# The last expert pass of a mixture-of-experts step: its gate and up products in two column halves, in two PSUM banks

## What is computed

```
h = silu(einsum('td,edf->tef', xf, w_gate)) * einsum('td,edf->tef', xf, w_up)
h = h * gates[..., None]              # gates: two of 32 experts for each token
y = einsum('tef,efd->td', h, w_down)  # f = 256, d = 1024
yp = rms_norm(yp + y, norm_f)         # and the same for the sample rows
```

## Time and profile before

| | us |
|---|---|
| median of 3 runs (613.83 to 614.82) | 614.73 |
| the profiled execution, its whole time | 613.61 |
| its span in the trace (first to last instruction) | 612.0 |
| TensorE busy in the span | 587.9 |
| last pass, first gate and up product | 577.30 |
| copy of the last pass's output (`yo`) begins | 590.10 |
| last scaling on VectorE begins | 608.05 |

### The profile page before, as it was taken

How to read it: one execution, slowest core, us unless ns; L and a number is a source line. 1 busy time by engine, 2 the same in 40 slices (tenths; PEclk the granted TensorE clock), 3 DMA queues, 4 the chain that set the end, 5 groups by cost and what they waited for, 6 DMA issues and landing times.

```text
span 612.0 us, 9005 instructions
## 1 busy us (share of the span) xinstructions
PE 587.9 (96%) x2880; PEld 350.1 (57%) x2880; DVE 322.5 (53%) x725; ACT 234.5 (38%) x415; POOL 52.6 (9%) x126
## 2 busy tenths in 40 slices
PE   7999999999999999999999989999999998999985
PEld 4876796867777686777656744343333333333331
DVE  4648788867767686767735873531141111121137
ACT  6451417275664737475535340211111211112224
POOL 1200001000000000000000002131112121121100
PEclk9999999999999999999999999999999999999999
DMA  8431308922223133221299989999999999999995
GB/s 315 137 137 71 138 34 323 408 104 69 77 77 103 43 103 109 71 77 69 79 331 391 384 348 322 364 419 419 419 418 421 419 421 419 421 420 417 415 370 222
DMA packets 34412, 157.65 MB, mean 258 GB/s; under 512 B 6480, under 2 KB 6864, under 8 KB 22992
## 3 DMA queue, kind: packets, MB, share of 16 engines
q1 hardware_dynamic: 28768, 146.51, 61.0%
q0 software_dynamic: 5472, 10.63, 4.7%
q10 hardware_dynamic: 144, 0.15, 0.1%
HBM read 151.87 MB, written 14.17 MB: 271 GB/s over the span
## 4 chain that ended last, share of the span: by engine, by line
PE 76%; DMA 10%; DVE 6%; ACT 3%; SPq 2%; issue 2%; DVEq 0%; ACTq 0%; POOLq 0%
PE ps L2099 14%; PE ps L1680 14%; PE ps L1682 13%; PE ps L1681 13%; PE ps L2128 8%; DMA wslot<-in_wmoe 5%; PE ps L1821 2%; PE ps L1856 2%; DMA raw<-in_wmix 2%; DMA gy<-ytok 1%; SPq L574 1%; PE ps L1803 1%; DMA ytok<-yo,idx 1%; PE ps L1847 1%; DVE wl L1031 1%
## 5 line engine op out<-in xcount | busy, mean ns | idle before, releaser
L2099 PE MATMUL ps<-wslot,xgT 128*64 128x512 f32 x520 | 116.7, 593 | 2.3 <-DMA wslot<-in_wmoe 1.9
L1680 PE MATMUL ps<-xh,wh 128*128 128x512 f32 x256 | 102.5, 400 | 0.0
L1682 PE MATMUL ps<-xl,wh 128*128 128x512 f32 x256 | 99.9, 390 | 0.0
L1681 PE MATMUL ps<-xh,wl 128*128 128x512 f32 x256 | 99.9, 390 | 0.0
L770 ACT ACTIVATE wh<-raw 128x1024 fp32r<-128x1024 f32 x48 | 50.7, 1059 | 120.5 <-PE ps L1682 101.1
L2099 PEld LDWEIGHTS ps<-wslot,xgT 128*64 128x64 f32 x520 | 37.8, 137 | 74.5 <-issue 73.7
L1031 DVE TENSOR_TENSOR wl<-raw,wh 128x1024 fp32r<-128x1024 f32 x48 | 58.6, 1222 | 23.8 <-ACT wh L770 22.5
L2128 PE MATMUL ps<-wslot,hT 128*64 128x512 f32 x272 | 62.2, 599 | 2.6 <-ACT hT L981 1.5
L1580 DVE SCALAR_TENSOR_TENSOR hm<-ps,rt,hs 128x128 f32<-128x128 f32 x24 | 7.3, 347 | 105.0 <-ACT hs L978 105.0
L1680 PEld LDWEIGHTS ps<-xh,wh 128*128 128x128 f32 x256 | 48.1, 188 | 16.1 <-issue 6.7
L1682 PEld LDWEIGHTS ps<-xl,wh 128*128 128x128 f32 x256 | 48.0, 188 | 10.6
(11 more groups left out here) (379 smaller groups left out, 837.4 us busy)
## 6 DMA issues: line engine op xcount, KB each, us to landing
wslot<-in_wmoe SPq DMA_DIRECT2D x87, 1024.0 KB, 18.4
raw<-in_wmix SPq DMA_DIRECT2D x56, 512.0 KB, 4.0
wslot<-in_wmoe SPq DMA_DIRECT2D x8, 512.0 KB, 20.2
gy<-ytok SPq DMA_DIRECT2D x8, 512.0 KB, 8.6
xt<-in_x SPq DMA_DIRECT2D x4, 512.0 KB, 7.8
at<-in_wmoe SPq DMA_DIRECT2D x2, 1024.0 KB, 18.9
x<-in_x SPq DMA_DIRECT2D x4, 512.0 KB, 4.4
xnd<-x SPq DMA_DIRECT2D x4, 512.0 KB, 9.6
```

The lines of the kernel that those rows point to most:

```text
L1680: pe.matmul(out, sh, mh_, start=start, stop=False)
L1681: pe.matmul(out, sl, mh_, start=False, stop=False)
L1682: return pe.matmul(out, sh, ml_, start=False, stop=stop)
L2099: l = pe.matmul(ps[CAP * s:CAP * s + CAP, 2, :], xgT[:, c, CAP * s:CAP * s + CAP], first_at[s * 4 + c] if first_at and c < 4 else at0[:, c ...
```

## The change

For the last pass alone, `pair` is replaced by a function of its own, `last_pair`. Its gate and up products come as two groups: first, for all 8 blocks c, the 128 gate and 128 up columns of f = 0, into bank 3; then for all 8 blocks those of f = 1, into bank 2. Each product has 256 moving columns (two runs of 128 of the weights' rows) in place of 512, and `gu_mm` is signalled after each group. ScalarE takes silu of 128 columns after each group, VectorE gates 128 columns after each. The transpose of the first `hm` half stands between blocks 5 and 6 of the second group, that of the second half between the two column halves of down's f = 0.

```diff
@@ ScalarE
-            expert_pass(nx + (PAIRS - 1), rtx[:, bass.ds(nx + (TAIL - 1), 1)])
+            a.activation(warm[:], ones[:, 0:1], ACT.Silu)
+            for f in range(2):
+                c = slice(f * P, f * P + P)
+                a.wait_ge(gu_mm, nx + (PAIRS + f))
+                a.sem_inc(held, 1)
+                a.activation(hs[:, c], ps[:, HT_BANK[f], 0:P], ACT.Silu, scale=rtx[:, bass.ds(nx + (TAIL - 1), 1)]).then_inc(silu_done, 1)
+            for f in range(2):
+                a.wait_ge(hT_mm, nx * 2 + (PAIRS * 2 - 1 + f))
+                a.activation(hT[:, f, :], ps[:, HT_BANK[f], 0:P], ACT.Copy).then_inc(hT_sb, 1)
+            a.wait_ge(pair_mm, nx + PAIRS)
+            a.wait_ge(y_out, nx * 16 + 16 * PAIRS)
+            a.activation(yo[:], ps[:, 6:8, :].rearrange("p b c -> p (b c)"), ACT.Copy).then_inc(yo_sb, 1)
@@ VectorE
-            gated(nx + (PAIRS - 1), rtx[:, bass.ds(nx + (TAIL - 1), 1)])
+            for f in range(2):
+                c = slice(f * P, f * P + P)
+                d.wait_ge(silu_done, nx + (PAIRS + f))
+                d.scalar_tensor_tensor(out=hm[:, c], in0=ps[:, HT_BANK[f], P:2 * P], scalar=rtx[:, bass.ds(nx + (TAIL - 1), 1)],
+                                       in1=hs[:, c], op0=ALU.mult, op1=ALU.mult).then_inc(hm_ready, 1)
@@ TensorE, in place of pair(nx + (HEAD + 3), 0, (use + 16, use + 16), False, (use, use))
+                pe.wait_ge(hm_ready, FIRST + G * 2)
+                pe.wait_ge(xgT_sb, FIRST + G + 1)
+                pe.wait_ge(hT_sb, FIRST + G * 2)
+                begin(PE_BANK)
+                for f in range(2):
+                    for c in range(KT):
+                        for s in range(2):
+                            if f == 0 and c == 0:
+                                pe.wait_ge(part_in[0][0][s], use)
+                            if f == 0 and c == 4:
+                                pe.wait_ge(part_in[1][0][s], use + 16)
+                            if f == 0 and c == 6:
+                                pe.wait_ge(last_gu_in[s], 16)
+                        if f == 1 and c == 6:
+                            hidden_T(0)
+                        for s in range(2):
+                            o = c * 512
+                            l = pe.matmul(ps[CAP * s:CAP * s + CAP, HT_BANK[f], 0:2 * P].rearrange("p (w c) -> p w c", w=2),
+                                          xgT[:, c, CAP * s:CAP * s + CAP],
+                                          wslot[0][s][:, o:o + 512].rearrange("p (w c) -> p w c", w=2)[:, :, f * P:f * P + P],
+                                          start=c == 0, stop=c == KT - 1, tile_position=(0, CAP * s), skip_group_check=True)
+                    l.then_inc(gu_mm, 1)
+                pe.wait_ge(hT_sb, FIRST + G * 2 + 1)
+                for s in range(2):
+                    pe.wait_ge(part_in[2][0][s], use + 16)
+                pe.wait_ge(yo_sb, FIRST + G)
+                down(0, 0)
+                hidden_T(1)
+                down(0, 1)
+                pe.wait_ge(hT_sb, FIRST + G * 2 + 2)
+                for s in range(2):
+                    pe.wait_ge(last_in[s], 16)
+                down(1, 0)
+                down(1, 1).then_inc(pair_mm, 1)
```

More of the change, by code:

```diff
@@ L2083, in pair @@
                 pe.wait_ge(hm_ready, FIRST + G * 2)
-                if not next_rows:
-                    pe.wait_ge(xgT_sb, FIRST + G + 1)
-                    begin(PE_BANK)
                 for c in range(KT):
@@ L2094, in pair @@
                             pe.wait_ge(part_in[c // 4][q][s], 32 if first_pass and c and s == 0 else (weights_in if c else half_in)[s])
-                    if c == 6 and not next_rows:
-                        for s in halves:
-                            pe.wait_ge(last_gu_in[s], 16)
                     for s in halves:
@@ L2121, in pair @@
                         pe.wait_ge(hT_sb, FIRST + G * 2 + 2)
-                    if f == 1 and not next_rows:
-                        for s in halves:
-                            pe.wait_ge(last_in[s], 16)
                     for h in range(2):
@@ L2164, in _, with last_pair, hidden_T, down @@
             pair(nx + (HEAD + 1), 1, (use, use), True)
+            def last_pair(G):
+                def hidden_T(f):
+                    pe.wait_ge(hm_ready, FIRST + G * 2 + (f + 1))
+                    pe.transpose(ps[:, HT_BANK[f], 0:P], hm[:, f * P:(f + 1) * P], ident[:]).then_inc(hT_mm, 1)
+                def down(f, h):
+                    for s in range(2):
+                        o = GU + f * D + h * 512
+                        l = pe.matmul(ps[CAP * s:CAP * s + CAP, 6 + h, :], hT[:, f, CAP * s:CAP * s + CAP],
+                                      wslot[0][s][:, o:o + 512], start=f == 0, stop=f == 1,
+                                      tile_position=(0, CAP * s), skip_group_check=True)
+                    return l
+                pe.wait_ge(hm_ready, FIRST + G * 2)
[28 more added lines that the diff above has]
+                pe.wait_ge(hT_sb, FIRST + G * 2 + 2)
+                for s in range(2):
+                    pe.wait_ge(last_in[s], 16)
+                down(1, 0)
+                down(1, 1).then_inc(pair_mm, 1)
@@ L2165, in _ @@
             pair(nx + (HEAD + 2), 2, (nx * 16 + kept_in,) * 2, True)
-            pair(nx + (HEAD + 3), 0, (use + 16, use + 16), False, (use, use))
+            last_pair(nx + (HEAD + 3))
             def last_rows(t):
```

## The result

| | before | changed |
|---|---|---|
| median of 22 runs | 614.79 us | 616.25 us |
| lowest to highest | 613.83 to 616.57 | 614.07 to 619.64 |
| ratio, 95% interval | | 1.0022 [1.0012, 1.0031] |
| the profiled execution | 613.61 | 617.77 |

Slower by 0.22%, some 1.4 us. A ratio here is taken from the single runs of both kernels, so it need not be the quotient of the two medians.

What follows compares the result with a forecast made beforehand. The chain's end was held by scatter and read back, the last pass 0.86 us early beside them. Stream +2.35, gap -1.0, transpose +0.15 put `yo` 1.4 us later and the end +0.45: 614.73 + 0.45 = 615.2 us, range 614.0 to 616.2.

Steps and rivals of the forecast that it cites:

- Off the chain, with slack: Last pass beside scatter and read back: 0.86 us early, delay free to some 0.95 us, an earlier end worth nothing.
- Weights land when they landed, and the first group waits 1.7 us for blocks 6 and 7: TensorE, last pass: landing times unchanged, first column group stops 1.7 us to 582.1, stream ends 2.35 us later.
- Rounds of 0.214 us, weight loads hidden: TensorE's gate and up products: 256-column rounds take 0.214 us, 3.43 us per group, no weight loads exposed.
- The rival of exposed loads: Last pass's products: 137 ns of loads per round unhidden over 20 rounds, 2.7 us more, 617.9 us; chance 0.06.
- The sum, +0.45 us: End of kernel: stream +2.35, gap -1.0, second transpose +0.15; `yo` 1.4 us later, past the slack the end +0.45 us.
- The two transposes: TensorE: one before the stream's end, one inside down, 0.14 us each or less, +0.3 us together.
- Silu to down: Between stream's end and down: silu of 128 columns 0.38 us, `hT` copy 0.27, 0.06 to TensorE.
- Down to `yo`: Down products to the copy of `yo`: second transpose adds 0.15 us, old weight slip goes, `yo` begins at 591.5.
- the slip of 0.1: Down's second half: its old wait for weights until 587.9, some 0.1 us, would go, since now wanted at 589.3.
- The base: Starting time for the whole kernel: median 614.73 us, the profiled execution of 613.61 lying 1.1 us below it.
- The clock, costed at nothing: TensorE's granted clock stays 1.00 through the new 1.7 us pause at 580.4, no longer than an earlier one.
- The hidden case: Rival at the last pass's end: weights 0.5 us earlier or read back 0.5 later, delay inside slack, 614.7 us; chance 0.22.

Runs made afterwards that it cites:

- the later sets: Three later sets of 12 runs of the changed kernel without an edit, against the kernel before: 615.14, 615.53 and 615.59 us, ratios 1.0005, 1.0014 and 1.0002.
- the two versions whose last pass isn't late: Changed kernel, blocks 4 to 7 using weights of blocks 0 to 3: 614.97 us; changed kernel, both column groups inside blocks landing together: 614.46, then 614.98 us.
- c0_before_again: The kernel before, without an edit, run again for a second profile: median 615.42 us, ratio 1.0000; profiled execution 615.03 us.
- the waits alone: Kernel before, last pass's waits for blocks 4 and 5 moved before block 2, for 6 and 7 before block 3: 616.01 us, 1.0013; again 615.87, 1.0021.
- without late weights: Changed kernel, blocks 4 to 7 multiplied with the weights of blocks 0 to 3, waits moved before down: 614.97 us, ratio 1.0004.
- with later ones: Changed kernel, SyncE requests blocks 6 and 7 of the last pass behind the first half of its down weights: 620.21 us, ratio 1.0084.

## Why the prediction was right, point by point

The direction and the mechanism came as told, the size did not quite. `yo` came 1.8 to 1.9 us later and the end 1.0 to 1.1, at the upper edge of the 1 to 1.8 and just past the 0.1 to 1.0 that had most of the chance; the median of 616.25 lies at the upper edge of the range (616.2). That the later sets (615.14 to 615.59) lie near the forecast of 615.2 is in part luck: the kernel before stood at 615.0 to 615.2 there and not at 614.73, and the change was put too low.

**Off the chain, with slack.** Right. In both profiles of the kernel before, and in the three of the two versions whose last pass isn't late, VectorE's fourth instruction is led by the read back. That an earlier `yo` is worth nothing was not tested by an earlier `yo` alone, since in both of those versions down's second half waits for weights until `yo` is as late as before.

**Weights land when they landed, and the first group waits 1.7 us for blocks 6 and 7.** Right: idle for 0.61 and 1.48 us in the rows of TensorE (some 0.16 less each than the pause, since a record lasts 0.38 us and the next round follows 0.214 after it), and 1.48 us over c0_before_again with the waits alone. This is the cause: without late weights the price is gone, with later ones it grows with them.

**Rounds of 0.214 us, weight loads hidden.** Right: 64 records in 7.13 us. The rival of exposed loads, 617.9, did not show: the same stretch holds 64 loads of 64 columns, 137 ns each, and nothing of them is added. The Trainium skill ("TensorE: Matmul & The Clock Gate", Part 3) lets a weight load overlap a running product only in other row groups; the trace disagrees with that here.

**The sum, +0.45 us.** Of the right sign, and too small: 1.0 to 1.1 us from the profiles. The step that failed in size is that of `yo`, "1.4 us later". Measured against the wait for blocks 6 and 7 it came 590.10 - 582.0 = 8.1 us behind it before and 595.11 - 585.1 = 10.0 us after: 1.9 us. The terms:
- The two transposes, put at 0.15 us each from eight in a row. Between products one costs 0.36: the last product ahead of it starts at 585.24 + 3.67 - 0.38 = 588.53, the next one at 589.10, 0.57 and not 0.21 later. Twice 0.21 us too little. That the row of eight hides the change of kind at its two ends is my reading; no run separates it.
- Silu to down: 0.71 us predicted, 590.33 to 590.91 measured, 0.13 less. The copy starts before the silu ends.
- Down to `yo`: 3.9 us predicted, 595.11 - 590.91 = 4.2 measured; 0.2 of it is the second transpose, counted above, and the slip of 0.1 that I took out stayed: 590.10 - 586.27 = 3.83 before, 4.20 - 0.36 = 3.84 after.
- These make 0.4 of the 0.5 us; a tenth is left without a term.

With 0.5 us more on `yo`, all past the slack, the sum would have read 0.95. The rest is the placing products, 2.05 us from start to VectorE where I had 1.95.

Against c0_before_again the sum closes: `yo` begins 595.11 - 580.12 = 14.99 us after F and there 13.20, so 1.79 later. The slack there was 0.71: tile 0's rows were ready at 592.83 + 2.05 = 594.88 (2.05 us as in the changed kernel, where VectorE waits for them), VectorE took them at 595.47, 0.59 later, and its next instruction stood another 0.12 behind (595.47 + 1.30 against 596.89). 1.79 - 0.71 = 1.08. The tail moved along, as said: from VectorE's fourth instruction to the end it is 617.77 - 599.64 = 18.13 us, and 615.03 - 596.89 = 18.14 in c0_before_again, though the chain now reaches the end over TensorE's sample products. The wait of ScalarE for the sample rows came where the text put it, 0.15 us.

**The base.** I added the change to the median of three runs, and the spread of F (4 us over the profiled executions) is larger than any term. In the first profile of the kernel before, unlike in the second, the first product did not wait, so the weights were on the early side there. The range had to hold that spread and did so narrowly.

**The clock, costed at nothing.** Right for the last pass of the changed kernel in all its profiles. The argument, though, one pause of 1.9 us without a drop, was too thin: the waits alone show a drop behind a shorter one.

**The rivals.** The hidden case had 0.22; two of the three later sets (1.0005 and 1.0002), alone, would look like it. The profiles say that it is not that.

## What to carry to other kernels

Splitting a product by output columns, so that each group runs over the whole contraction, makes the first group want all of the weights in half the time; where the weights arrive at the rate of the products, as here, the stream then ends half a stream behind the last landing. Split inside the blocks that land together, and ask what is queued behind the stall that is removed: here the read back, and the next weights, took all of it. Where runs spread by more than the effect, look for a mark in the profile that carries the spread, and compare what follows it, over several profiles of both kernels.

## What the runs showed of the hardware

- The time behind the landing of the last pass's first weights repeats to 0.01 us over four executions of one kernel, while the landing itself moves by 4 us.
- The granted clock can drop in one execution and not in the next of the same kernel, far from the stage in question: 0.50 for 3 to 7 us between 364 and 372 in three of four profiles of the changed kernel, 1.00 in the fourth and in both of the kernel before.
- Behind the same pause of 1.48 us TensorE's granted clock was 0.51 in one execution and 1.00 in another (and in the four profiles of the changed kernel, with the same pause, it stayed at 1.00 too); behind one of 4.49 us it was 0.50, and the products behind it took 5.94 us in place of 3.67.
- A single float32 transpose of 128x128 between float32 products of 64-column tiles takes 0.36 us of TensorE, against 0.14 in a row of eight.
- Two 64-column weight loads of 137 ns side by side stay hidden under rounds of 256 moving columns, 0.214 us each: 64 records in 7.13 us.
